# Block 2 mixing of a two-block transformer kernel: rotary key made with the gates, rotary partners as extra weight columns, latent keys two heads at a time

## The reference

```python
def rope(x, pos, rot_dim):
    ...
    x1, x2 = xr[..., :half], xr[..., half:]
    rot = jnp.concatenate([x1 * cos - x2 * sin, x2 * cos + x1 * sin], axis=-1)

def mla_attention(c_q, c_kv, k_rope, q_norm, w_uq, kv_norm, w_ukv, pos):
    q = (rmsnorm(c_q, q_norm) @ w_uq).reshape(b, s, MLA_HEADS, MLA_NOPE + MLA_ROPE)   # 6 heads, 64 + 32
    q_nope = q[..., :MLA_NOPE]
    q_pe = rope(q[..., MLA_NOPE:], pos, MLA_ROPE)
    kv = (rmsnorm(c_kv, kv_norm) @ w_ukv).reshape(b, s, MLA_HEADS, MLA_NOPE + MLA_V)  # 6 heads, 64 + 64
    k_nope, v = kv[..., :MLA_NOPE], kv[..., MLA_NOPE:]
    k_pe = rope(k_rope[:, :, None, :], pos, MLA_ROPE)[:, :, 0]
    # scores = (q_nope . k_nope + q_pe . k_pe) * scale, causal softmax, times v
```

## Time and profile before

| | us |
|---|---|
| median of 3 runs | 3536.68 |
| lowest, highest | 3535.44, 3541.72 |
| span of the profiled execution | 3539.9 |
| mixing part with latent steps and pairs, first layer | about 1869 to 2052 |
| the same, second layer | about 2959 to 3140 |

### The profile page before, as it was taken

One profiled execution on the slowest core, in us unless ns is written; L12 is line 12 of the kernel. 1 busy time (PEld: TensorE's weight loads), 2 busy tenths in 40 slices (PEclk: granted clock), 3 DMA queues, 4 the chain that ended last, 5 costly groups with the idle time before them and its releaser, 6 DMA issues.

```text
span 3539.9 us, 42333 instructions
## 1 busy us (share of the span) xinstructions
PE 3423.7 (97%) x15820; PEld 2664.3 (75%) x15820; DVE 1671.6 (47%) x2184; ACT 1228.0 (35%) x1833; POOL 210.7 (6%) x247
## 2 busy tenths in 40 slices
PE   9989999998899999999999999999999999999998
PEld 6657888775678887888776678887888776578887
DVE  6744443576354335443545654434443454654433
ACT  4333122432432224232454442233223344442223
POOL 2300000022010000000001310000000001300000
PEclk9999999999999999999999999999999999999999
DMA  6213322321233222332321043332332321023332
GB/s 166 60 48 72 95 95 98 91 79 42 60 95 97 95 95 77 98 98 95 84 60 30 17 98 95 100 96 89 95 96 100 90 72 35 12 81 99 95 96 71
DMA packets 418742, 288.92 MB, mean 82 GB/s; under 512 B 23632, under 2 KB 396540, under 8 KB 418376
## 3 DMA queue, kind: packets, MB, share of 16 engines
q1 hardware_dynamic: 415752, 280.74, 26.8%
q0 software_dynamic: 2736, 4.58, 0.8%
q10 hardware_dynamic: 144, 2.10, 0.2%
HBM read 285.25 MB, written 2.13 MB: 81 GB/s over the span
## 4 chain that ended last, share of the span: by engine, by line
PE 91%; DVE 4%; ACT 3%; issue 2%; DMA 0%; DVEq 0%; SPq 0%; ACTq 0%
PE bank L1921 27%; PE bank L1923 26%; PE bank L1922 26%; PE bank L1931 2%; PE bank L2063 1%; PE bank L2017 1%; PE bank L2039 1%; PE bank L2107 1%; PE bank L2403 1%; PE bank L2405 1%; DVE stat L1479 1%; PE bank L1970 1%; ACT whi L917 0%; PE bank L2141 0%; PE bank L1992 0%
## 5 line engine op out<-in xcount | busy, mean ns | idle before, releaser
L1921 PE MATMUL bank<-hh,whi 128*128 128x512 f32 x2848 | 1150.9, 404 | 45.6 <-DVE hl L1402 22.8
L1922 PE MATMUL bank<-hl,whi 128*128 128x512 f32 x2848 | 1117.1, 392 | 0.0
L1923 PE MATMUL bank<-hh,wlo 128*128 128x512 f32 x2848 | 1116.8, 392 | 0.0
L1352 DVE TENSOR_TENSOR wlo<-raw,whi 128x1024 fp32r<-128x1024 f32 (+2 forms) x536 | 644.5, 1204 | 337.5 <-ACT whi L917 323.5
L1921 PEld LDWEIGHTS bank<-hh,whi 128*128 128x128 f32 x2848 | 540.7, 190 | 197.6 <-issue 61.4
L917 ACT ACTIVATE whi<-raw 128x1024 fp32r<-128x1024 f32 (+2 forms) x536 | 547.8, 1032 | 250.9 <-PE bank L1923 250.4
L1922 PEld LDWEIGHTS bank<-hl,whi 128*128 128x128 f32 x2848 | 540.5, 190 | 122.4 <-issue 14.1
L1923 PEld LDWEIGHTS bank<-hh,wlo 128*128 128x128 f32 x2848 | 539.6, 189 | 114.6
L1921 PE MATMUL bank<-fshi,whi 128*128 128x512 f32 (+2 forms) x1364 | 529.3, 388 | 0.1
L1923 PE MATMUL bank<-fshi,wlo 128*128 128x512 f32 (+2 forms) x1364 | 525.2, 385 | 0.0
L1922 PE MATMUL bank<-fslo,whi 128*128 128x512 f32 (+2 forms) x1364 | 525.1, 385 | 0.0
(11 more groups left out here) (235 smaller groups left out, 2455.9 us busy)
## 6 DMA issues: line engine op xcount, KB each, us to landing
raw<-in_ffn_w_gate SPq DMA_DIRECT2D x88, 512.0 KB, 3.8
raw<-in_ffn_w_up SPq DMA_DIRECT2D x88, 512.0 KB, 3.8
raw<-in_ffn_w_down SPq DMA_DIRECT2D x88, 512.0 KB, 3.5
raw<-in_w_in SPq DMA_DIRECT2D x82, 512.0 KB, 3.9
raw<-in_w_up SPq DMA_DIRECT2D x64, 512.0 KB, 4.0
raw<-in_w_down SPq DMA_DIRECT2D x64, 512.0 KB, 3.4
raw<-in_w_out SPq DMA_DIRECT2D x16, 512.0 KB, 4.1
raw<-in_w_in SPq DMA_DIRECT2D x16, 256.0 KB, 3.6
```

The costliest lines, as they stand in the source:

```text
L1352: dve.tensor_tensor(slot3(wlo, s, m), slot3(raw, s, m), slot3(whi, s, m).bitcast(F32), ALU.subtract).then_inc(c.lo_done.sem, 1)
L1921: pe.matmul(o, wh, ah, start=start, stop=False)
L1922: pe.matmul(o, wh, al, start=False, stop=False)
L1923: return pe.matmul(o, wl, ah, start=False, stop=stop)
```

## The change

It does four things, in both layers of block 2.

1. The unit of the gates (64 columns) takes in the 32 columns of the rotary key, and again its two halves in swapped order. The product `gatesf` so gives gates in rows 0 to 63, the key in 64 to 95 and its partners in 96 to 127. Group `pe` with its unit, and `spe`, are gone.
2. The unit of `w_uq` is loaded with 128 columns a head: 96 of the head, and the last 32 in swapped halves. `mq` makes 128 rows; the six `sm` are gone.
3. The rotation reads the partner rows from SBUF (`rotate`, steps `key_pe` and `turn_q`) on 32 partitions; the sine table stands a second time in partitions 96 to 127. `key_pe` stands behind the second norm, `turn_q h` behind `mq h`.
4. `w_ukv` is loaded with all keys ahead of all values, so that three groups `mk` make the keys of two heads each; each is copied out in two halves.

```diff
+    t2[96:P, 1536:2048] = t2[64:96, 1536:2048]
-    fill.append(add("gatesf", "fm", ("w_in", 1568), frees="act", dst=M_POSX))
+    fill.append(add("gatesf", "fm", ("w_gates_pe", 0), frees="act", dst=M_POSX))
     latent += [("rn", "cq"), ("sq", "ckv")]
-    latent.append(add("pe", "fm", ("w_in", 320), frees="act", dst=M_PE, rows=(64, 96), after_norm=3, **late))
-    latent += [("mix", 0), ("mix", 1), ("rn", "ckv")]
-    latent.append(add("spe", "swap", None, of="pe", tile=M_PE, rows=(64, 96), perm="m", tab=1024, frees="dve", after_norm=4, **late))
+    latent += [("mix", 0), ("mix", 1), ("rn", "ckv"), ("key_pe",)]
...
-    first_pair = [query(0), query(1), ("g", "sm0"), key(0), ("g", "sm1"), key(1), value(0), value(1), value(2), value(3)]
-    second_pair = [query(2), key(2), ("g", "sm2"), query(3), key(3), ("g", "sm3")]
-    third_pair = [query(4), key(4), ("g", "sm4"), query(5), key(5), ("g", "sm5")]
+    first_pair = [query(0), query(1), ("turn_q", 0), key(0), ("turn_q", 1), value(0), value(1), value(2), value(3)]
+    second_pair = [query(2), ("turn_q", 2), key(1), query(3), ("turn_q", 3)]
+    third_pair = [query(4), ("turn_q", 4), key(2), query(5), ("turn_q", 5)]
...
+                elif kind == "w_gates_pe":
+                    src = w["w_in_2"][la, :, :].rearrange("a (k p) n -> p (a k) n", p=P)
+                    for at_, c0, n_ in ((0, 1568, 64), (64, 384, 32), (96, 400, 16), (112, 384, 16)):
+                        sp.dma_start(cols8[:, :, at_:at_ + n_], src[:, :, c0:c0 + n_]).then_inc(done, 16)
...
+                    for k_ in range(2):
+                        for at_, c0, n_ in ((0, 0, MLA_D), (96, 80, 16), (112, 64, 16)):
+                            sp.dma_start(uq[:, k_, :, at_:at_ + n_], src[:, k_, :, c0:c0 + n_]).then_inc(done, 16)
...
+                if kind == "ukv_k":
+                    act.activation(g(gr["dst"], S, (0, HD)), bk[0:HD, :], ACT.Copy).then_inc(c.act_step.next(), 1)
+                    act.activation(g(gr["dst"] + S, S, (0, HD)), bk[HD:P, :], ACT.Copy).then_inc(evac, 1)
...
+            def rotate(c, source, to, beside, done):
+
+                cos, sin = tab[64:96, 1024:1024 + S], tab[96:P, 1536:1536 + S]
+                dve.tensor_tensor(g(beside, S, (64, 96)), g(source, S, (96, P)), sin, ALU.mult).then_inc(c.dve_step.next(), 1)
+                dve.tensor_tensor(g(source, S, (64, 96)), g(source, S, (64, 96)), cos, ALU.mult).then_inc(c.dve_step.next(), 1)
+                dve.wait_ge(c.dve_step.sem, c.dve_step.now(l))
+                dve.tensor_tensor(g(to, S, (64, 96)), g(source, S, (64, 96)), g(beside, S, (64, 96)), ALU.add).then_inc(done.sem, 1)
...
+                    for head in range(2):
+                        dve.tensor_copy(g(gr["dst"] + S * head, S, (64, 96)), g(M_PE, S, (64, 96))).then_inc(c.kpe.sem, 1)
...
+                elif kind == "ukv_k":
+                    dve.tensor_copy(g(gr["dst"], S, (0, HD)), bk[0:HD, :]).then_inc(c.dve_step.next(), 1)
+                    dve.tensor_copy(g(gr["dst"] + S, S, (0, HD)), bk[HD:P, :]).then_inc(evac, 1)
```

More of the change, by code:

```diff
@@ L533, in build @@
                 last_of[wo + n_out - 2] += 1
-            loads = [2 if u[0] in ("w_in2", "w_in_halves", "w_late") else 3 if u[0] == "w_early" else 1 for u in units]
-            size = [{"w_uq": 576, "w_ukv": 768, "w_early": 640, "w_late": 768}.get(u[0], UNIT) for u in units]
+            loads = [{"w_in2": 2, "w_in_halves": 2, "w_late": 2, "w_ukv": 2, "w_early": 3, "w_gates_pe": 4, "w_uq": 6}.get(u[0], 1) for u in units]
+            size = [{"w_uq": 768, "w_ukv": 768, "w_early": 640, "w_late": 768}.get(u[0], UNIT) for u in units]
             blocks.append(dict(units=units, order=order, groups=groups, steps=steps, wo=wo, first=first, n=len(units),
@@ L2004, in pair @@
                         p = e["pair"]
[L2005 removed]
+                        need(c, b, l, f"mk{p}", *(f"mv{t}" for t in range(QT)))
                     if q >= 2:
```

72 lines of the change are left out of this document (46 added, 26 removed).

## The result

The changed kernel takes 3554.24 us (median of 5, 3550.36 to 3558.96), the kernel before 3536.68. The ratio is 1.0046 with a 95% interval of 1.0034 to 1.0058: 17.6 us slower, where 13 us faster was forecast, and outside the range of 3504 to 3533. The profiled execution has a span of 3554.5 us, 14.6 above that of before.

What follows compares the result with a forecast made beforehand. PE (97% busy) and DVE's queue were taken to bound the latent part by turns. Per layer 4.4 + 0.3 - 0.5 + 2.7 - 0.4 = 6.5 us, 13.0 in two, from 3536.7 to about 3524; range 3504 to 3533.

Steps and rivals of the forecast that it cites:

- What left PE: Matmuls, permutations, key groups and bank 7 waits removed from PE: 17.25 us per layer, 34.5 in both, as upper end.
- Stretch 1: From the norm's sum at 1893.62 to `mq0`: 4.4 us kept per layer.
- a later norm: Norm one attention step later: 10.9 us from its sum to entry 3's transposes instead of 10.2, 0.7 lost.
- Stretch 2: From `mq0` to the transposes at 1951.92: DVE's queue is the bound at 14.7 us, 0.3 kept per layer.
- Stretch 3: From `mq2` to the transposes at 1983.77: `mq3` waits for `mk1`'s DVE work, a loss of 0.5 us per layer.
- Stretch 4: Entries 27 to 33: PE is the bound, 3.7 us removed, 2.7 kept per layer.
- Two SBUF inputs: Rotation steps meeting POOL's scalings: 0.43 us a meeting, one on the path, 0.4 lost per layer.
- Rival 2: DVE and POOL block each other in the rotations: 3535 if all 14 steps meet, 3529 if half; chance 0.15.
- Rival 1: PE is all that counts and DVE has slack: 3508, or 3502 with all removed work kept; chance 0.2.
- Rival 3: Longer PE waits drop its clock to 1.2 GHz; three more falls per layer give 3544; chance 0.05.
- The loads: Gates' unit load, issued at 1792.90 and split at 1820.66, stays hidden by 27.8 us of cover; `w_uq` hidden too.

Runs made afterwards that it cites:

- e14: e9 with the six query rotations moved later in DVE's queue: 3514.89 us, ratio 0.9933 to the kernel before.
- e1: Kernel before with the gates' part alone (rotary key in the gates' unit, no `pe`/`spe`, norm one step later): 3525.63 us.
- e13: Changed kernel with its six query rotations moved later in DVE's queue, the order of PE, ACT and POOL unchanged: 3522.73 us.
- e6: Kernel before with two-head keys, a PE product of constants in each of the three places left by removed key products: 3541.49 us.
- e12: e10 with three products of constants on PE in front of the transposes that wait behind the first norm: 3530.42 us.
- e18: e14 with the product `ckv` moved behind attention step 6 and its square behind step 7: 3514.01 us.
- e4: Changed kernel with six products of constants per layer on PE, in front of four waits for DVE's copy: 3547.23 us.
- e9: Changed kernel with three empty steps holding the removed key products' places, so other steps keep their gaps: 3538.77 us.
- e8: Changed kernel with the queries put back to 96 rows and permutations on PE: 3541.53 us.
- e10: e8 with empty steps holding the three removed key products' places: 3530.68 us.
- e2: Kernel before with the queries' part alone (128 rows, rotated from SBUF), later pairs' rotations ahead of keys: 3538.64 us.
- e7: Changed kernel with the keys put back to one head per product, later pairs' rotations ahead of keys: 3528.34 us.

## Why the prediction was wrong

**What left PE (34.5 us): the list was right, its worth was not.** With rotations late and places kept (e14) the change is worth 24 us. That is more than my 13. The forecast erred on the order, not on the work.

**Stretch 1: right in the first layer, too high in the second.** Forecast 4.4 kept, measured 5.4 and 2.0; a wait of 3.6 us behind the norm, measured 3.75. The one hidden danger, a later norm, was priced well: 10.9 us for the same work, measured 2.30 + 8.66 (1894.29 to 1896.59, then to 1905.25). e1 shows that the lead lasts. The prediction took the second layer to be like the first; there the kernel before needs 2.9 us less from the first scores to those of entry 38, and I didn't look for the reason.

**Stretch 2: the step that failed.** I summed DVE's queue to 14.7 us and took 0.3 as kept. It took 17.7 (1931.57 to 1949.26), and 17.7 again in the second layer (3028.66 to 3046.35). The difference of 3.0 is on the lines above: 1.66 idle for the scores that now stand behind `mq0` and `mq1` in one gap; 0.5 more of waiting for ACT's high half (2.00 instead of the 1.5 that I carried over from before); and 0.66 because the two rotations took 0.84, 0.93, 0.68, 0.69, 1.04, 0.68 instead of 6 x 0.70. Together 2.8. A sum of durations assumes that the queue always has something ready. I had the waits of the old order in it and did not make the new order's; that is the term that was mis-sized. e13 bears this out. Its stretch has no rotation in it, so my sum would be 14.7 - 4.2 = 10.5, and from `hl` to the end of the last copy DVE takes 13.2 (1924.13 to 1937.35): 2.7 too much again, with waits of 1.64, 0.94 and 2.13 in it. So it is the waits and not the rotations that the sum had wrong, and the rotations come on top because DVE is the bound there.

**Stretch 3 (-0.5 forecast, -3.8 measured).** The places I named were right: `mk1` with two copies on DVE, and `mq3` waiting for it (1.66 us, from the trace after). What was missing is that `turn_q3` stands in front of the maximum of entry 26 and so of the copy for the transposes at 1984.92, which wait 2.54. The wait for ACT's high half is 2.00 here too (1976.96).

**Stretch 4 (+2.7 forecast, -4.7 measured).** More than half of these 7.4 us is the clock. Between the transposes that end stretch 3 and the scores of entry 28 the same work takes 2.87 us before (1983.77 to 1986.64) and 5.25 after (1984.92 to 1990.17): 2.4 us at half speed, where PE is the bound. To the transposes behind those scores it is 3.0 (3.85 against 6.87 us).

```profile
1986.64 1.03 PE L2017 MATMUL bank<-G 96*128 96x256 f32 x4
```

This is the line of before; 1990.17 of after is shown above. A second fall stands behind the wait at 2011.74: from there to the fourth matmul of `out0` it is 3.7 us, before it is 2.2, so 1.5 more. Between the scores of entries 28 and 34 PE now has three waits of 1.05, 0.57 and 1.52 us instead of one of 0.78. The last of the three, behind DVE's copy, is gone in e13. That "PE is the bound there" was true of a queue without rotations in front of maxima.

**Two SBUF inputs (-0.4): small, as forecast, if not as small.** The long steps coincide with POOL: the cosine step of 1.04 us at 1945.41 begins 0.5 us before this scaling ends, which by itself takes 1.31:

```profile
1944.17 1.74 POOL L905 TENSOR_SCALAR G<-G,stat 128x384 f32<-128x384 f32 x2 [3.75 <-DVE stat L1496]
```

The 14 cosine steps have a mean of 0.82 us in the changed kernel, the sine steps 0.71. The excess over 0.69 is about 1 us per layer, 0.66 of it in stretch 2. In e13 two steps of 1.15 us stand in a narrow entry and cost nothing that can be seen. Rival 2 (3529 to 3535) is not what happened.

**Rival 1 (PE is all, 3502 to 3508)** comes true in parts only: in e6, with the places kept, PE's added work cost its whole length; behind the norm nothing that PE did counted (e12, e18).

**Rival 3 (the clock, 3544, chance 0.05)** had the sign and much of the size. The granted clock over two stretches of 160 us, one per layer (column before the DMA share), before and then after:

```profile
1880.00:2040.00 160.00, 150.00 (x951) 96.31 (x950) 90.96 (x154) 72.31 (x199) 44.59 (x72) 0.97 0.08 22
2970.00:3130.00 160.00, 149.12 (x960) 95.31 (x958) 91.91 (x156) 71.57 (x195) 45.01 (x72) 0.99 0.08 25
```

```profile
1880.00:2040.00 160.00, 135.91 (x867) 88.86 (x866) 88.68 (x148) 68.20 (x191) 42.56 (x69) 0.93 0.06 18
2970.00:3130.00 160.00, 136.30 (x863) 89.62 (x863) 88.53 (x148) 67.40 (x186) 40.83 (x66) 0.93 0.08 21
```

From these means, 0.04 x 160 + 0.06 x 160 = 16 us of PE's full-speed time are missing, nearly the whole loss. That is an upper bound for the cost, as an estimate from rounded means: a fall at the norm costs 0.1 us (e12), the one behind 1984.92 costs 2.4 to 3.0 (e4 and stretch 4). The rival's chance was too low by the prediction's own rows. It held that waits of 0.54 and 0.68 leave the clock up, and passed over the wait of 0.94 at 1926.28 in the earlier trace rows, behind which eight transposes take 1.75 us where eight take 1.04 at the higher clock. But the falls follow from the order in DVE's queue: e13 changes nothing on PE, and the means go back to 0.97 and 0.98. How the 17.6 us split between waits and half-speed work was not measured apart.

**The loads: right.** The gates' unit was issued at 1792.91 and split at 1820.65, before at 1792.90 and 1820.66, with no wait in front of it.

What stays open is why the queries' and keys' parts cost 13 us more together than apart. Both e9 and e13 lie below the changed kernel, so places and rotations each carry more than the surplus, and I can't say how it divides. One candidate was not run: where the queries' part is added with rotations in the gaps of the permutations it costs about 13 us (e8 to the changed kernel) or 8 (e10 to e9), and where it is added with rotations and keys of the later pairs exchanged, it costs about 1 (e2) or 3 (e1 to e7).

## What to carry to other kernels

Where an even spread of steps sets the order, removing a step moves all the others; hold its place open, or print the new order and walk each in-order queue with its waits, not with a sum of durations. A step that nobody needs soon (here a rotation needed ten entries later) belongs behind the narrow pieces of the engine that makes others wait, and not in front of a maximum or copy that the bound engine needs next. Before paying to keep PE's clock up, look at who ends the next wait: where it was another engine's copy, the slow clock cost 0.1 us (e12), and where it was PE itself, 2.4 (e4).
